# A two-layer hybrid trunk on one core: layer 1's first norm turned tile by tile, and half of layer 0's second norm placed inside the output projection

## The reference

```
a = modulate(rmsnorm(h), sh_a, sc_a)         # first norm ("a")
mix = concat(retention(a), ssd(a), neighbourhood_attention(a))   # via one input projection
h = h + g_a * (mix @ w_out)
f = modulate(rmsnorm(h), sh_f, sc_f)         # second norm ("f")
h = h + g_f * moe_ffn(f)                     # 16 experts, top 2 in the best of 4 groups
```

## Time and profile before

| what | value |
| --- | --- |
| runs | 1301.29 us median of 3 (1298.95 to 1301.44) |
| the profiled execution | 1300.2 us, its span 1298.4 us |
| mean granted TensorE clock | 0.953 |
| TensorE busy | 1156.4 us, 89% of the span |
| VectorE, ScalarE, GpSimd busy | 425.1, 217.5, 138.4 us |
| transfers | 318.88 MB |
| matmuls of the input projection by tiles (L846) | 480, 186.9 us |

### The profile page before, as it was taken

How to read it: one execution, slowest core, us unless ns; L and a number is a source line. 1 busy time by engine, 2 the same in 40 slices (tenths; PEclk the granted TensorE clock), 3 DMA queues, 4 the chain that set the end, 5 groups by cost and what they waited for, 6 DMA issues and landing times.

```text
span 1298.4 us, 17851 instructions
## 1 busy us (share of the span) xinstructions
PE 1156.4 (89%) x7368; PEld 652.2 (50%) x7368; DVE 425.1 (33%) x803; ACT 217.5 (17%) x415; POOL 138.4 (11%) x122
## 2 busy tenths in 40 slices
PE   3899998999999579999999279998999769999876
PEld 1444444676654335654564045554765345655543
DVE  0140123794322641212121423024732352222113
ACT  2120221112220411110110222122121211101100
POOL 0002101650000100000000200211400000000001
PEclk8999999989999889999999689999998979999999
DMA  9421115642370578999997542135627569999997
GB/s 382 152 85 65 66 65 194 236 187 84 124 311 1 195 289 340 399 426 424 426 425 285 180 153 83 65 120 219 222 85 304 217 237 377 400 424 427 427 427 296
DMA packets 35056, 318.88 MB, mean 246 GB/s; under 512 B 7072, under 2 KB 8224, under 8 KB 17312
## 3 DMA queue, kind: packets, MB, share of 16 engines
q1 hardware_dynamic: 22432, 292.03, 56.2%
q0 software_dynamic: 5472, 12.59, 2.8%
q10 hardware_dynamic: 7072, 13.11, 2.8%
HBM read 310.89 MB, written 14.16 MB: 250 GB/s over the span
## 4 chain that ended last, share of the span: by engine, by line
PE 78%; DMA 11%; DVE 7%; ACT 2%; issue 2%; SPq 0%; POOL 0%; DVEq 0%; ACTq 0%; POOLq 0%
PE ps L846 14%; PE ps L1189 13%; PE ps L1090 6%; PE ps L833 6%; PE ps L1221 6%; PE ps L1192 4%; DMA ring<-in_w_mod 3%; DMA arena<-in_w_down 3%; PE ps L779 3%; PE ps L1195 2%; PE ps L1003 2%; DMA arena<-in_w_gate 2%; PE ps L1230 2%; PE ps L1166 2%; PE ps L1019 2%
## 5 line engine op out<-in xcount | busy, mean ns | idle before, releaser
L846 PE MATMUL ps<-ring,featT 128*128 128x512 f32 (+1 forms) x480 | 186.9, 550 | 0.0
L846 PEld LDWEIGHTS ps<-ring,featT 128*128 128x128 f32 x480 | 90.7, 190 | 92.3 <-issue 89.9
L1189 PE MATMUL ps<-arena 128*64 128x256 f32 x896 | 104.2, 386 | 5.9 <-ACT arena L1518 2.4
L2072 DVE TENSOR_TENSOR arena<-arena,ps 128x256 f32<-128x256 f32 (+2 forms) x32 | 15.6, 488 | 222.2 <-PE ps L1189 111.1
L1189 PEld LDWEIGHTS ps<-arena 128*64 128x64 f32 x896 | 64.5, 139 | 43.3 <-issue 15.5
L1090 PE MATMUL ps<-ring,featT 128*128 128x512 f32 x192 | 82.7, 592 | 0.0
L833 PE MATMUL ps<-featT,ring 128*128 128x512 f32 (+1 forms) x192 | 80.5, 577 | 2.3 <-ACT featT L1343 2.3
L2332 POOL DMA_INDIRECT arena<-ffn_rows,slot_i x26 | 26.3, 1013 | 486.1 <-DVE slot_i L2007 461.4
L1525 ACT ACTIVATE arena<-ps 128x256 f32<-128x256 f32 (+2 forms) x32 | 14.0, 438 | 310.1 <-PE ps L1189 143.7
L1192 PE MATMUL ps<-arena 128*128 128x512 f32 x128 | 58.3, 611 | 2.3 <-ACT arena L1518 2.3
L1090 PEld LDWEIGHTS ps<-ring,featT 128*128 128x128 f32 x192 | 36.6, 191 | 46.4 <-issue 46.4
(11 more groups left out here) (313 smaller groups left out, 1638.0 us busy)
## 6 DMA issues: line engine op xcount, KB each, us to landing
ring<-in_w_mod SPq DMA_DIRECT2D x21, 2048.0 KB, 8.4
arena<-in_w_up SPq DMA_DIRECT2D x20, 2048.0 KB, 16.9
arena<-in_w_gate SPq DMA_DIRECT2D x16, 2048.0 KB, 16.3
ring<-in_w_down SPq DMA_DIRECT2D x12, 2048.0 KB, 13.4
arena<-in_w_down SPq DMA_DIRECT2D x12, 2048.0 KB, 17.5
ring<-in_w_in SPq DMA_DIRECT2D x10, 2048.0 KB, 8.0
ring<-in_w_gate SPq DMA_DIRECT2D x8, 2048.0 KB, 17.5
ring<-in_w_out SPq DMA_DIRECT2D x4, 2048.0 KB, 8.4
```

What stands on the lines that cost most here:

```text
L846: o = mm(bank[:, lo:hi], featT[:, k, P * i:P * i + P], W[:, k, lo:hi], start=k == 0, stop=k == KD - 1)
L1189: o = mm(ps[64 * half:64 * half + 64, m, 0:256], X_[:, k, at:at + SMALL_CAP], W[:, k, 256 * half:256 * half + 256], start=k == 0, stop=k = ...
```

## The change

Three edits. In layer 1's first norm TensorE turns tile by tile (`tiles_turned`), each as soon as it is normalised, into all eight banks: context tiles in banks 0 to 3, latent tiles in banks 4 to 7, two feature blocks to a bank; ScalarE evicts blocks 0, 1, 4, 5 and VectorE 2, 3, 6, 7, the context half first. In the input projection, in both layers, the wait for all evictions goes and one stands before each of the first job's eight blocks. In the second norm each tile group is squared, scaled and multiplied inside the residual (`norm_group`), and in layer 0 the sixteen context transposes stand before the last tile's output projection (`context_turned`, banks 0 to 3, two blocks to a bank) with their eight evictions beside it (`context_evac`); the second gate rows wait for these. Behind the gate rows only the latent tiles are turned. In layer 1, which has no context there, only the first of these moves applies. The counts of the semaphores `f_tr`, `f_evac`, `f_evac_dve`, `f_ms` and `f_rs` follow (in the table, in `router`, in `turn_back` and in GpSimd's loop over `f_groups`; not shown).

```diff
@@ -485,6 +485,14 @@
+        def f_groups(l):
+            return [[0, 1], [2], [3]] if l < DEPTH - 1 else [[2], [3]]
+        def f_turned(l):
+            return KD if l < DEPTH - 1 else 0
         def norm_groups(ts):
...
@@ -795,24 +803,33 @@
+            def tiles_turned(l):
+                for t in range(NT):
+                    pe.wait_ge(S("a_hn"), upto("a_hn", l, t + 1))
+                    for k in range(KD):
+                        c = CTX * (k % 2) + P * (t % 2)
+                        i = tr(ps[:, 4 * (t // 2) + k // 2, c:c + P], tokA[:, t, P * k:P * k + P], ident)
+                        if t % 2 == 1 and k % 2 == 1:
+                            i.then_inc(S("a_tr"), 1)
             def norm_transpose(l, which, ts, blocks=range(KD)):
-                pe.wait_ge(S(which + "_hn"), upto(which + "_hn", l, len(ts)))
+                pe.wait_ge(S(which + "_hn"), upto(which + "_hn", l, len(ts) if which == "a" else len(tiles(l))))
                 if which == "f":
...
                         name = which + ("_evac" if k % 2 == 0 else "_evac_dve")
-                        pe.wait_ge(S(name), upto(name, l, (k - 4) // 2 + 1))
+                        ahead = f_turned(l) // 2 if which == "f" else 0
+                        pe.wait_ge(S(name), upto(name, l, ahead + (k - 4) // 2 + 1))
                     for j, t in enumerate(ts):
...
                 jobs = in_jobs(l)
-                pe.wait_ge(S("a_evac"), upto("a_evac", l, KD // 2))
-                pe.wait_ge(S("a_evac_dve"), upto("a_evac_dve", l, KD // 2))
                 for n, (name, kind, i, _) in enumerate(jobs):
...
@@ -830,6 +847,10 @@
                         for k in range(KD):
+                            if n == 0:
+                                of_act = (k if l == 0 else k // 2) % 2 == 0
+                                evac = "a_evac" if of_act else "a_evac_dve"
+                                pe.wait_ge(S(evac), upto(evac, l, k // 2 + 1 if l == 0 else 2 * (k // 4) + k % 2 + 1))
                             o = mm(bank[:, lo:TOK], W[:, k, c:c + P], featT[:, k, lo:TOK],
...
@@ -1082,6 +1103,8 @@
                 for t in ts:
+                    if f_turned(l) and t == ts[-1]:
+                        context_turned(l)
                     for half in range(N_OUT):
...
@@ -1092,11 +1115,25 @@
+            def context_turned(l):
+                pe.wait_ge(S("row0"), upto("row0", l, len(segs(l))))
+                pe.wait_ge(S("f_hn"), upto("f_hn", l, 2))
+                for k in range(KD):
+                    for t in range(2):
+                        c = 256 * (k % 2) + P * t
+                        i = tr(ps[:, k // 2, c:c + P], tokA[:, t, P * k:P * k + P], ident)
+                    if k % 2 == 1:
+                        i.then_inc(S("f_tr"), 1)
             def gate_rows(l, which):
...
                     pe.wait_ge(S("row0"), upto("row0", l, len(segs(l))))
+                    if f_turned(l):
+                        pe.wait_ge(S("f_evac"), upto("f_evac", l, f_turned(l) // 2))
+                        pe.wait_ge(S("f_evac_dve"), upto("f_evac_dve", l, f_turned(l) // 2))
                 for seg in segs(l):
...
@@ -1105,8 +1142,8 @@
                 ts = tiles(l)
-                pe.wait_ge(S("f_evac"), upto("f_evac", l, KD // 2))
-                pe.wait_ge(S("f_evac_dve"), upto("f_evac_dve", l, KD // 2))
+                pe.wait_ge(S("f_evac"), upto("f_evac", l, (KD + f_turned(l)) // 2))
+                pe.wait_ge(S("f_evac_dve"), upto("f_evac_dve", l, (KD + f_turned(l)) // 2))
                 pe.wait_ge(S("ld_rw"), 16)
...
@@ -1288,14 +1325,17 @@
             for l in range(DEPTH):
-                norm_transpose(l, "a", range(NT), range(4 if l == 0 else 0, KD))
+                if l == 0:
+                    norm_transpose(l, "a", range(NT), range(4, KD))
+                else:
+                    tiles_turned(l)
                 project(l)
...
                 gate_rows(l, 1)
-                norm_transpose(l, "f", tiles(l))
+                norm_transpose(l, "f", [2, 3])
                 router(l)
...
@@ -1329,16 +1369,34 @@
                     elif which == "f":
-                        act.wait_ge(S("res_dve"), upto("res_dve", l, N_OUT * (t - ts[0] + 1)))
+                        act.wait_ge(S("res_dve"), upto("res_dve", l, N_OUT * (t - tiles(l)[0] + 1)))
                     A(tokA[:, t, :], h[:, t, :], ACT.Square, accum_out=stat[:, t:t + 1]).then_inc(S(which + "_sq"), 1)
+            def context_evac(l):
+                act.wait_ge(S("modA"), upto("modA", l + 1, 1))
+                for k in (0, 1, 4, 5):
+                    act.wait_ge(S("f_tr"), upto("f_tr", l, k // 2 + 1))
+                    A(featT[:, k, 0:CTX], ps[:, k // 2, 256 * (k % 2):256 * (k % 2) + CTX], ACT.Identity,
+                      scale=modA[:, l, 1, k, 0:1], bias=mod[:, l, 24 + k, 0:1]).then_inc(S("f_evac"), 1)
...
                 act.wait_ge(S("modA"), upto("modA", l + m, 1))
+                if which == "a" and l > 0:
+                    for seg in range(2):
+                        for k in (0, 1, 4, 5):
+                            act.wait_ge(S("a_tr"), upto("a_tr", l, 4 * seg + k // 2 + 1))
+                            c = slice(CTX * seg, CTX * seg + CTX)
+                            i = A(featT[:, k, c], ps[:, 4 * seg + k // 2, CTX * (k % 2):CTX * (k % 2) + CTX], ACT.Identity,
+                                  scale=modA[:, l, m, k, seg:seg + 1], bias=mod[:, l, 24 * m + k, seg:seg + 1])
+                            if seg == 1:
+                                i.then_inc(S("a_evac"), 1)
+                    return
                 for k in range(0, KD, 2):
-                    act.wait_ge(S(which + "_tr"), upto(which + "_tr", l, k + 1))
-                    for seg in (segs(l) if which == 'f' else [0, 1]):
+                    act.wait_ge(S(which + "_tr"), upto(which + "_tr", l, (f_turned(l) // 2 if which == "f" else 0) + k + 1))
+                    for seg in ([1] if which == "f" else [0, 1]):
                         c = slice(CTX * seg, CTX * seg + CTX)
...
@@ -1585,7 +1643,10 @@
                 gate_rows(l, 0)
-                square_rows(l, "f", tiles(l))
+                square_rows(l, "f", tiles(l)[:-1])
+                if f_turned(l):
+                    context_evac(l)
+                square_rows(l, "f", tiles(l)[-1:])
                 gate_rows(l, 1)
...
@@ -1648,9 +1709,19 @@
                 dve.wait_ge(S("modA"), upto("modA", l + m, 1))
+                if which == "a" and l > 0:
+                    for seg in range(2):
+                        for k in (2, 3, 6, 7):
+                            dve.wait_ge(S("a_tr"), upto("a_tr", l, 4 * seg + k // 2 + 1))
+                            c = slice(CTX * seg, CTX * seg + CTX)
+                            i = V.tensor_scalar(featT[:, k, c], ps[:, 4 * seg + k // 2, CTX * (k % 2):CTX * (k % 2) + CTX], modA[:, l, m, k, seg:seg + 1],
+                                                mod[:, l, 24 * m + k, seg:seg + 1], ALU.mult, ALU.add)
+                            if seg == 1:
+                                i.then_inc(S("a_evac_dve"), 1)
+                    return
                 for k in range(1, KD, 2):
-                    dve.wait_ge(S(which + "_tr"), upto(which + "_tr", l, k + 1))
-                    for seg in (segs(l) if which == "f" else [0, 1]):
+                    dve.wait_ge(S(which + "_tr"), upto(which + "_tr", l, (f_turned(l) // 2 if which == "f" else 0) + k + 1))
+                    for seg in ([1] if which == "f" else [0, 1]):
                         c = slice(CTX * seg, CTX * seg + CTX)
...
@@ -1922,6 +1993,28 @@
                         n += 1
+                    for m, group in enumerate(f_groups(l)):
+                        if group[-1] == t:
+                            norm_group(l, m, group)
+                    if f_turned(l) and t == ts[-2]:
+                        context_evac(l)
+            def norm_group(l, m, group):
+                a = slice(group[0], group[-1] + 1)
+                dve.wait_ge(S("f_sq"), upto("f_sq", l, group[-1] - tiles(l)[0] + 1))
+                V.tensor_scalar(stat2[:, a], stat[:, a], 1.0 / D, EPS, ALU.mult, ALU.add).then_inc(S("f_ms"), 1)
+                dve.wait_ge(S("f_rs"), upto("f_rs", l, m + 1))
+                for t in group:
+                    V.tensor_scalar(tokA[:, t, :], h[:, t, :], stat2[:, t:t + 1], None, ALU.mult).then_inc(S("f_hn"), 1)
+            def context_evac(l):
+                dve.wait_ge(S("modA"), upto("modA", l + 1, 1))
+                for k in (2, 3, 6, 7):
+                    dve.wait_ge(S("f_tr"), upto("f_tr", l, k // 2 + 1))
+                    V.tensor_scalar(featT[:, k, 0:CTX], ps[:, k // 2, 256 * (k % 2):256 * (k % 2) + CTX],
+                                    modA[:, l, 1, k, 0:1], mod[:, l, 24 + k, 0:1], ALU.mult, ALU.add).then_inc(S("f_evac_dve"), 1)
...
@@ -2230,7 +2323,6 @@
                 residual(l)
-                norm_rows(l, "f", tiles(l))
```

(8 more changed lines are left out.)

## The result

| | before | after |
|---|---|---|
| median of 20 runs, us | 1302.6 (1298.2 to 1334.7) | 1293.28 (1289.8 to 1300.4) |
| ratio, 95% interval | | 0.9924 (0.9911 to 0.9938) |
| profiled execution, its span, us | 1300.2, 1298.4 | 1291.35, 1289.5 |

The change is faster by 0.76%, some 10 us. Two further sets of the same kernel gave 0.9914 and 0.9919, so the size holds. (Now and then an execution of any of these kernels takes some 30 us longer at a lower granted clock, such as the one of 1334.7; ratios and means leave these out.)

A forecast was written before the change was run, and what follows sets the result against it. It took TensorE to bound the kernel (78% of the span, transfers 11%). Terms of 1.3 + 3.4 + 0.6 = 5.3 us, taken from the median 1301.29, gave 1296.0 us, range 1293.6 to 1299.7.

The forecast's parts named there:

- layer 0, waits per block: Layer 0's input projection starts right behind the last transpose, no longer waiting for the last evictions: 1.3 us gained.
- layer 1's first norm: Transposes start 2.05 us earlier, tile by tile, and 1.35 us of evictions are no longer waited for: 3.4 us gained.
- layer 0's second norm: Inserted transposes cost 1.7 us, fewer at the end give 2.26 back, an earlier last tile 0.1: net 0.6 us gained.
- layer 1's second norm: Only one product leaves its end, where it lay beside the last rsqrt: zero gain.
- the gate rows' copy as the next stall: Layer 0's second norm: transposes also wait for ScalarE's gate-row copy (end 429.23), so the earlier last tile buys at most 0.1 us.
- the two lags I had: TensorE's clock rose 3.0 us after transposes began in layer 0's first norm and 5.7 us after in layer 1's.
- Everything behind the three places starts with TensorE: Stages and weight loads behind the three edited places start earlier along with TensorE, so the 5.3 us sum reaches the end.
- early rise: Rival: in layer 1's first norm the clock rises 3.0 us after the transposes' start; gain 6.7 us, 1294.6; chance 0.15.
- the gain stays upstream: Rival: expert-weight loads near the end hold the gain, 1301.3, or partly, or a clock fall costs 3 us, 1299; chance 0.18.
- The projection at half rate: Rival: layer 1's first two projection jobs run at half clock after the earlier start; slower, for example 1305.1; chance 0.04.

The follow-up runs named there:

- kept busy: Before and after with unread constant-tile transposes put into TensorE's waits; ratios to before 0.9928 (1295.2 us) and 0.9890 (1290.45 us).
- the waits alone: Before with only the input projection's waits changed to one per block of the first job, old norm order kept; ratio to before 0.9971, 1299.6 us.
- the tile order alone: Before with only layer 1's first norm turned by tiles through eight banks, waits before the whole job kept; ratio to before 0.9989, 1302.2 us.
- before with the delay of 1.8 us: Before with 16 constant-tile transposes ahead of the sixth job of layer 0's input projection; ratio to before 0.9991, 1302.55 us.
- the delays: 16 or 32 constant-tile transposes ahead of layer 0's sixth projection job; before took 1302.55 and 1306.7 us, after 1297.8 and 1299.4.
- unchanged copy: Before, instruction for instruction, as a second copy with no change; ratio to before 0.9975 (0.9958 to 0.9991), 1301.05 us.
- the fourth set: Runs of before and after, each with 16 or 32 constant-tile transposes ahead of layer 0's sixth projection job; ratios to before 0.9991, 1.0029, 0.9962, 0.9976.

## Why the prediction was too small

**The edited places** can be read in every trace. The third column has means over the sixteen profiled executions that were not kept busy, with and without each edit. For the last column I take out of each stretch what half clock cost in it, as an estimate: half of the time that TensorE worked there at 0.50, since the same work takes about twice as long (0.195 and 0.108 us for a transpose).

| term | forecast | measured, mean | at equal clock |
|---|---|---|---|
| layer 0, waits per block (end of the modulation to the fourth job) | 1.3 | 1.4: 23.1 to 21.7 | 1.3: 20.4 to 20.5 in eight traces, 19.1 in eight |
| layer 1's first norm (first product to the fourth job) | 3.4 | 3.5: 20.6 to 17.2 | 3.0: 18.0 to 18.1 without either part, 15.0 with both |
| layer 0's second norm (output projection to router) | 0.6 | 0.5 to 0.7: 69.30 to 68.76 in most | 0.55: 69.30 to 68.75 |
| layer 1's second norm (output projection to router) | 0 | 0.85: 38.82 to 37.97 | 0.44: 4.89 to 4.45 from the gate rows to the transposes |

In the two executions of the tables above the first term can't be seen: start to states took 209.03 and 209.11 us, because the clock rose at 42.4 before, but at 44.9 after, when the projection had begun at half rate. At equal clock the four terms give 1.3 + 3.0 + 0.55 + 0.44 = 5.3 us, the forecast's sum. That the sum agrees so well is luck in part: one term was 0.4 too large and one 0.44 too small. In the third each piece held: 1.75 us for the inserted transposes (I took 1.7), 5.21 - 2.92 = 2.29 back (2.26), and the gate rows' copy as the next stall. In the second the start came 2.0 us earlier (I took 2.05), but the projection still began 0.3 us behind the last transpose, so that of the 1.35 of evictions 1.0 came back. That its mean is 3.5 is the clock, which in the profiled execution of after rose 4.3 us after the transposes began, between the two lags I had. The tile order and the waits both counted, since either alone left the projection slower (with the waits alone 18.1, with the tile order alone 18.5 us to the fourth job).

**"Layer 1's second norm only loses one product from its end ... Zero"** is a step that failed, and a small one. I took the earlier product to lie beside the rsqrt and so to be free. It lay beside it and made it slower: before, then after.

```profile
1025.20 0.74 DVE L1644 TENSOR_SCALAR tokA<-h,stat 128x1024 f32<-128x1024 f32 x1
1025.36 0.99 POOL L2252 TENSOR_TENSOR stat<-stat,pw 128x1 f32<-128x1 f32 x1 [0.75 <-DVE stat L1639]
```

```profile
1015.70 0.55 POOL L2344 TENSOR_TENSOR stat<-stat,pw 128x1 f32<-128x1 f32 x1 [13.18 <-DVE stat L2006]
1016.29 0.75 DVE L2009 TENSOR_SCALAR tokA<-h,stat 128x1024 f32<-128x1024 f32 x1 [0.66 <-POOL stat L2344]
```

It took 0.99 us in all nine profiled kernels without the second norm's edit and 0.55 in all nine with it: the 0.44. The rest of the 0.85 is not the edit but the clock at two places of this stage: the gate rows ahead of the output projection, and the last transposes. Here are the gate rows before and after, and the transposes after (the earlier trace rows has those of before).

```profile
991.47 3.52 PE L1102 MATMUL ps<-arena,const 128*128 128x512 f32 x4
```

```profile
983.31 2.03 PE L1139 MATMUL ps<-arena,const 128*128 128x512 f32 x4
...
1017.10 3.12 PE L828 MATMUL ps<-const,tokA 128*128 128x128 f32 x16 [2.58 <-DVE tokA L2009]
```

From these gate rows to the output projection it takes 1.8 to 2.0 us in four traces and 3.2 to 3.4 in the others, and one of the four is before with the delay of 1.8 us, which has none of the edits. In the same four the last transposes and evictions take 3.8 to 4.1 us up to the router, as against 2.95 or 3.4.

**"Everything behind the three places starts with TensorE"** is the step that cost most, with the sum that follows from it: it has no term for stages without an edit. It was true of when stages start and not of how long they last. The edits are worth 5.3 us at equal clock and the kernel gained 10, so some 4.8 us are missing from the sum. Three profiled executions each of before and of after, 10.2 us apart in their mean spans, show where. The stages with an edit differ by 6.5, 1.2 more than at equal clock. The others differ by 3.6: 2.2 in layer 0's attention and the output's transposes, 0.8 between states and attention, 0.7 up to the last expert, 0.5 in layer 1 from projection to output's transposes, less 0.7 that was lost from layer 1's router to the end (and 0.1 elsewhere).

Why these stages are shorter stays open. The granted clock is what the runs point at. In the same executions TensorE worked at half clock for 59, 69 and 62 us before and for 52, 48 and 51 after, 13 less in the mean, and what takes 13 us at half clock takes 6.5 less at full. Over all runs the mean clock is 0.957 for after and 0.951 for before, each 0.001 of it goes with 0.73 us, and at equal mean clock the difference is 6.4 us (5.7 to 7.1). That is a correlation; a kernel with fewer standstills also has a higher mean clock by that alone. What makes the clock fall less often in the changed kernel, an edit at its place or the shift of what lies behind, the delays were to show and did not.

I saw this possibility only in part. The rival "early rise" was about one place in layer 1's norm and gave 1294.6, nearer to the result than my forecast; the rise there came half early, and was worth 0.7 of its 1.4. The rival "the gain stays upstream" had a fall of the clock in another sparse stretch, but as a loss of 3 us, never as a gain. I ought to have asked the same, in both directions, of every place where the view of the earlier trace rows shows the clock to fall, and to have made the range wider on both sides.

**The starting point** hid a part of the miss: I subtracted from 1301.29, the median of three. Over 20 runs it was 1302.6, and the same sum would have given 1297.3, further from the result.

**The other rivals.** The projection at half rate did not come in layer 1: the clock had risen (751.5) before it began (753.03). The gain did not stay upstream: the two pieces of expert weights moved with the rest.

## What to carry to other kernels

Work the edited places out from the rows; here this was right to 0.1 us in two of four and to 0.45 in the others, once the clock was taken out. Then list where TensorE falls to half clock, in several executions of the same kernel, and put into the range, on both sides, what these places cost: here stages without an edit made 3.6 of 10 us. Measure an unchanged copy before you read a small difference between two kernels; here it came out 2.8 us off, and four pure delays, which are one small edit each, could not be read against it. And an operation "beside" another is free only if the two don't slow each other: look for the same operation alone, elsewhere in the trace.

## What the runs showed of the hardware

- GpSimd's rsqrt of 128 values took 0.55 us with VectorE idle, 0.99 beside one VectorE product from and to SBUF, and 1.28 beside three in a row. In the last two cases it was over only after a product had ended (1026.35, the product 1025.94; 428.00, the second of three 426.56 + 2 x 0.68 = 427.92). The Trainium skill, in "SBUF — State Buffer", on the two sides of SBUF, says that GpSimd and, in some of its modes, VectorE share a port pair that whichever starts first holds for its whole instruction. The trace agrees in direction; no run here tells that lock from another cause.
- Whether TensorE fell to half clock in a given sparse stretch differed between executions of one program: at the end of layer 0's attention in two of three of before, for some 10 us, at a price of 3.3 (attention and the output's transposes took 59.9 us with it and 56.6 without).
- The clock's place alone moved a stretch by more than an edit did: four gate-row matmuls took 3.36 us up to the next matmul at half clock (before) and 1.86 where the clock had risen among them (after).
- Extra transposes of a constant tile in TensorE's waits, which compute nothing, made before 0.7% faster. At full clock a 128x128 transpose took 0.111 us (16 in 1.78, in the fourth set).
- The Trainium skill, in "TensorE: Matmul & The Clock Gate", on the HAM clock gate, says that the count of slow matmuls differs from run to run of one kernel, and puts the penalty of the ramp below 1% of a span. Here TensorE's work at half clock was 59 to 69 us in three executions of before. By the same halving, the 10 us between them cost some 5, 0.4% of the span: small by that measure, and yet half of what was to be measured.
